# Hybrid attention and SwiGLU block on one core: attention steps of the first three groups taken in pairs on TensorE

## The chip, the cores and the metric

The kernel runs on one core of one Trainium2 chip. The metric is device time in microseconds (us) of that core. The changes are judged against the median of three runs of the kernel before, and the profile is one execution of the program on the chip.

## What is computed

The reference applies one layer to `x` (512 tokens, 2048 features): a sparse attention mixer with a residual, then a SwiGLU feed-forward with a residual. Cut to what matters here:

```python
h = rms_norm(x, norm_mix_g)
proj = h @ w_in                       # 16 query heads of 128, 6 x 4 key/value heads, gates
for each group g of 4, each of its 4 heads, each branch (selected, window), each tile of 128 queries:
    s = q @ k.T * scale               # causal, so tile t has (t + 1) * 128 keys
    p = softmax(masked s) * gate
    o += p @ v                        # the compressed branch is added to the same sum
x = x + concat(o) @ w_out
h = rms_norm(x, norm_ffn_g)
x = x + (silu(h @ w_gate) * (h @ w_up)) @ w_down
```

With 512 tokens all 8 selection blocks are taken, so the selected branch is plain causal attention with its own keys and values. A product in float32 is written as three products of float32r parts: `mm3` multiplies high by high, high by low and low by high part.

## The kernel before

Five engines run their own programs, written out by hand and bound together by semaphores. TensorE (PE) does all products and the transposes, ScalarE (ACT) makes the high parts (`copy`), the exponentials and the copies of results, VectorE (DVE) makes the low parts (`lo`), maxima and weights, SyncE (SP) loads the weights, GpSimd (POOL) takes inverse roots.

The attention part runs over four groups, and each group over 32 steps (`STEPS`), i = 0 to 31: head i // 8, branch i // 4 % 2, query tile t = i % 4. The names used below, for step i:

- **S(i)**, `scores(i)`: the product of queries and keys into PSUM bank 2 + i % 2, three matmuls of 256 to 512 columns. For t = 0 one call serves both branches, so S(i) with i % 8 == 4 issues nothing.
- **max(i)**, `maximum(i)` on DVE: mask, maximum and a copy into `pbuf` (two halves, i % 2). **exp(i)**, `probs(i)` on ACT: the exponential in `pbuf` and its row sum. **weigh(i)**, `weigh(i)` on DVE: three small instructions on `wgt` and `pbuf`, which let the transposes go (`p_ready`).
- **T(i)**, the transposes on PE: t + 1 tiles of `pbuf` into bank 4 + i % 2, in full float32.
- **pth(i)** on ACT and **ptl(i)** on DVE, both named `pt_part(i)`: high and low part of the transposed tiles. Where t = 0 and i is 4 or more, pth(i) waits for `pv_done`, since the values of the branch before still read the buffer `pth`.
- **V(m)**, `values(m)` on PE: the products with the values for the four tiles of branch m, 12 matmuls and one more for an even m.
- **F(w)**, `filler(w)`: in the first three groups half a unit of the next group's projection, which gives PE work while the other engines run. A half with w of 8 or more is 12 matmuls of 512 columns. The table `FILL_P` gives them to the steps. Steps with i % 4 == 1 (from 5 on) have none: V(i // 4 - 1) stands there.
- `keys_sums`, `keys_bcast`, `queries_sums`: the norms of the next group's keys and queries, issued at the steps `KSUM_AT`, `KB_AT`, `KB2_AT`, `QSUM_AT`. DVE takes the results in `keys_den`, `keys_diag`, `keys_norm` and `queries_den`, one step off these.

On PE a step is: V if i % 4 == 1, the fillers, at i % 8 == 0 four transposes of `pc` (compressed branch), T(i), S(i + 2), then sums or broadcasts. On DVE the turn i of the loop is: weigh(i - 1), at i % 8 == 2 a part of `ptc`, ptl(i - 2), max(i), at i % 8 == 7 a product for the compressed branch (`compressed_thrice`), outputs of the projection and a weight split (`splits`). On ACT it is: exp(i), pth(i - 1), the same outputs and splits. Each engine runs its list in order, so an instruction that waits holds all behind it. ptl(i) also waits until S(i + 2) is done.

The two lines that set who waits for the values are in ACT's `pt_part`:

```python
if i >= TT and i % TT == 0:
    wait(act, pv_done, i // TT, 2 * REP, g)
```

Of the kernel before, what the change touches and what calls it, by code (L numbers as in the profile page):

```python
# [4 lines left out]
P = 128  # L5
S, D = 512, 2048
HEADS, GROUPS, DH = 16, 4, 128
REP = HEADS // GROUPS
CMP_LEN, CMP_STRIDE = 32, 16
N_CMP = (S - CMP_LEN) // CMP_STRIDE + 1  # L10
CPAD = 32
# [6 lines left out]
TT = S // P  # L18
# [107 lines left out]
LAST = GROUPS - 1  # L126
# [12 lines left out]
    + [[42], [43], [], [], [44], [45]]  # L139
TAIL_A, END_A = [46], 47  # L140

KSUM_AT, KB_AT, KB2_AT, QSUM_AT, KSPLIT_AT = 13, 17, 19, 26, STEPS - 2


assert S // SEL_BLOCK <= N_SELECT and WINDOW >= S
# [4 lines left out]
def nsa_swiglu_block(nc, x, mix_g, ffn_g, w_in, b_gate, q_g, k_g, cmp_pos, cmp_w1, cmp_b1, cmp_w2,  # L150
# [5 lines left out]
    with ctx:  # L156
# [104 lines left out]
        def bank(b):  # L261
            return ps[:, b, :]
# [58 lines left out]
        def wait(eng, s, base, per=0, i=0):  # L321

            eng.wait_ge(s, i * per + base if per else base)
# [30 lines left out]
                self.local, self.per, self.i = 0, 0, 0  # L354

        WARM = 14
        H_BANKS = [0, 1, 2, 3, 4, 5, 6, 7, 2, 3, 4, 5, 6, 7, 2, 3]
# [654 lines left out]
        def _(dve):  # L1014
# [211 lines left out]
            def attention(g, fill, tail, last):  # L1226
# [90 lines left out]
                def maximum(i):  # L1317
                    nk = (i % TT + 1) * P
                    e, m = slice(i % 2, i % 2 + 1), i // (2 * TT) * TT + i % TT
                    first = 0 if i % TT else (2 + i // TT % 2) * P  # L1320
                    nc.vector.tensor_tensor_reduce(pbuf[:, i % 2, 0:nk], bank(2 + i % 2)[:, first:first + nk], causal[:, S - nk:],  # L1321
                                                   nrq[:, m:m + 1], 3e38, ALU.add, ALU.min, nb[:, e]).then_inc(nb_ready, 1)
# [27 lines left out]
                    for q in range(3, OWN // 2):  # L1350
                        first_out(q)
                for i in range(1, STEPS + 2):
                    if i <= STEPS:
                        weigh(i - 1)
                    if i % 8 == 2:
                        wait(dve, ptc_hi, i // 8 + 1, REP, g)
                        at = ptc[2 * CPAD:, :]
                        lo(at, bank(0)[2 * CPAD:3 * CPAD, :], at, ptc_ready)
                    if i >= 2:
                        pt_part(i - 2)  # L1360
                    if i < STEPS:
                        maximum(i)
                    if i == 1:
                        compressed_weigh()
                        splits(ended(HEAD_FILL))
                    if i % 8 == 7 and i < STEPS - 1:
                        compressed_thrice(i // 8 + 1)
                    if i < 2:
                        continue
                    j = i - 2  # L1370
                    if last and j:
                        staged_added(after(j - 1))
                    if last and j >= 8 and j % 8 == 0:
                        dve.wait_ge(own_hi, j // 8)
                        lo(hTl[:, OWN + j // 8 - 1, :], bank(1), hTh[:, OWN + j // 8 - 1, :], own_lo)
                    if not last:
                        for part, half in part_halves(fill, j):
                            part_out(g + 1, part, half)
                    splits(after(j))
                    if last:  # L1380
                        continue
                    if j == 3:
                        dve.wait_ge(cs_done, g + 1)
                        compressed_keys(g + 1)
                    if j == KSUM_AT - 1:
                        keys_den(g + 1)
                    if j == KSUM_AT:
                        keys_diag(g + 1)
                    if j == KB_AT - 1:
                        keys_norm(g + 1, 0)  # L1390
                    if j == KB2_AT - 1:
                        keys_norm(g + 1, 1)
                    if j == QSUM_AT - 1:
                        queries_den(g + 1, 0)
                    if j == KSPLIT_AT:
                        keys_split(g + 1)
# [275 lines left out]
        def _(pe):  # L1672
            def mm(out_, a, b, start=False, stop=False):
                return nc.tensor.matmul(out_, a, b, start=start, stop=stop, skip_group_check=True)  # L1674
# [160 lines left out]
            def keys_sums(p):  # L1835

                wait(pe, ksq_ready, 2, 2, p)
                for j in range(8):
                    last = mm(bank(0)[:, j:j + 1], sq[:, j // TT, j % TT * P:(j % TT + 1) * P], inv128[:, 0:1], True, True)
                last.then_inc(ksum_done, 1)  # L1840

            def keys_bcast(p, b):

                wait(pe, kdiag_ready, 1, 1, p)
                if b:
                    wait(pe, k_norm, 1, 2, p)
                for t in range(TT):
                    last = mm(bank(0)[:, t * P:(t + 1) * P], inv128[:, :], diag[:, b * TT + t, :], True, True)
                last.then_inc(kb_done, 1)

            def queries_sums(p, h0):

                wait(pe, qsq_ready, h0 + 2, 4, p)
                for h in (h0, h0 + 1):
                    for t in range(TT):
                        last = mm(bank(0 if h0 == 0 else 5)[:, h * TT + t:h * TT + t + 1], sq[:, h - h0, t * P:(t + 1) * P],
                                  inv128[:, 0:1], True, True)
                last.then_inc(qsum_done, 1)
# [26 lines left out]
            def attention(g, fill, tail, last_group):  # L1885
# [54 lines left out]
                def filler(w, tiles=(0, 1)):  # L1940
                    u, half = w // 2, w % 2
                    if u == 0:
                        wait(pe, q_lo, 3 + half, 4, g)
                    if not last_group:
                        proj_half(u, half, P_UNITS, g + 1, g + 1)
                        return
                    c, q = u // 3, u % 3
                    if half == 0 and 0 in tiles:
                        arrive(A0 + u)
                        if c == 0:  # L1950
                            pe.wait_ge(ot_lo, 2 * q + 2)
                    if q == 0 and c:
                        pe.wait_ge(x2_staged, 2 * (c - 1) + half + 1)
                    tokens_half(A0 + u, q, half, 6 + half, 12, tiles)
# [10 lines left out]
                compressed_scores()  # L1965
                for w in HEAD_FILL[0 if last_group else 2:]:
                    filler(w)
                for i in range(STEPS):
                    t = i % TT
                    if i > TT and t == 1:  # L1970
                        values(i // TT - 1)
                    for w in fill[i]:
                        filler(w)
                    if last_group and i == STEPS - 1:
                        filler(tail[0], (0,))
                    if i % 8 == 0:
                        h = i // 8
                        wait(pe, pc_ready, h + 1, REP, g)
                        if h:
                            wait(pe, ptc_ready, h, REP, g)  # L1980
                        if not last_group and h == 2:
                            wait(pe, k_den, 1, 1, g + 1)
                        if not last_group and h == 3:
                            wait(pe, k_norm, 2, 2, g + 1)
                        for tt in range(TT):
                            last = nc.tensor.transpose(bank(0)[0:3 * CPAD, tt * P:(tt + 1) * P],  # L1986
                                                       pc3[:, tt, :, :].rearrange("p r c -> p (r c)"), ident[:, :])
                        last.then_inc(trc_done, 1)
                    wait(pe, p_ready, i + 1, STEPS, g)
                    if i == 1:  # L1990
                        wait(pe, q_den, 2, 2, g)
                    if i >= 2:
                        wait(pe, pt_lo, i - 1, STEPS, g)
                    for k in range(t + 1):
                        ks = slice(k * P, (k + 1) * P)
                        last = nc.tensor.transpose(bank(4 + i % 2)[:, ks], pbuf[:, i % 2, ks], ident[:, :])  # L1996
                    last.then_inc(tr_done, 1)
                    if i + 2 < STEPS:
                        scores(i + 2)
                    if last_group:  # L2000
                        continue
                    if i == KSUM_AT:
                        wait(pe, ptc_ready, KSUM_AT // 8 + 1, REP, g)
                        keys_sums(g + 1)
                    if i == KB_AT:
                        wait(pe, ptc_ready, KB_AT // 8 + 1, REP, g)
                        keys_bcast(g + 1, 0)
                    if i == KB2_AT:
                        keys_bcast(g + 1, 1)
                    if i == QSUM_AT:  # L2010
                        wait(pe, ptc_ready, QSUM_AT // 8 + 1, REP, g)
                        queries_sums(g + 1, 0)
                for w in tail:
                    filler(w, (1,) if last_group else (0, 1))
                values(2 * REP - 1)
# [136 lines left out]
```

## Time and profile before

| | |
|---|---|
| time, median of 3 runs | 2195.71 us (2193.26 to 2196.3) |
| profiled execution: its own time | 2192.59 us |
| profiled execution: span | 2190.6 us |
| PE busy | 2176.8 us (99%) |
| DVE busy | 1557.3 us (71%) |
| ACT busy | 1038.0 us (47%) |
| mean granted TensorE clock | 0.997 |

The span runs from the first to the last instruction. The steps of attention run from about 260 to 850 us, some 145 us for a group. A busy PE is not a PE at its peak: matmuls overlap, so a record is longer than the time until the next one starts. What a matmul costs in a stream is the distance between two starts. A releaser in brackets names the instruction that ended an idle time.

### The profile page before, as it was taken

To read this page: it belongs to the slowest core of one execution; us is meant where nothing else is said; L and a number is where in the kernel's file an instruction comes from. 1 tells how busy PE (TensorE), PEld (TensorE's weight loads), DVE (VectorE), ACT (ScalarE), POOL (GpSimd) and SP (SyncE) were. 2 spreads that over 40 slices of the span, in tenths; PEclk is the share of its full clock that TensorE was granted. 3 is DMA by queue.
4 is the path that set the end of the run, shared out by engine and by line. 5 is a ranking of instruction groups with operands and counts; after the bars stand their busy time and mean duration, and the time that the engine had idled before them with its cause. 6 is when DMAs were issued, how large, how long until landed. Compare 5 with 4: busy or idle time off the path is not lost.

```text
span 2190.6 us, 30130 instructions
## 1 busy us (share of the span) xinstructions
PE 2176.8 (99%) x11377; PEld 1867.0 (85%) x11377; DVE 1557.3 (71%) x2261; ACT 1038.0 (47%) x1482; POOL 101.1 (5%) x115
## 2 busy tenths in 40 slices
PE   9999999999999999999999999999999999999999
PEld 7898988989889998788888888888888888888887
DVE  6333466575666554798777777777877898989898
ACT  5332345343444333864445445445444565555553
POOL 1000000000001000100000000000000000000000
PEclk9999999999999999999999999999999999999999
DMA  5342212212214222644655555455465677666545
GB/s 177 116 116 87 78 59 59 68 49 67 60 59 145 68 68 81 208 164 122 179 162 161 154 165 178 120 163 178 131 175 163 185 225 237 192 192 197 174 143 164
DMA packets 209071, 300.49 MB, mean 137 GB/s; under 512 B 16588, under 2 KB 116209, under 8 KB 207521
## 3 DMA queue, kind: packets, MB, share of 16 engines
q1 hardware_dynamic: 197522, 255.40, 35.8%
q0 software_dynamic: 11408, 43.20, 9.5%
q8 instruction: 90, 1.47, 0.3%
q14 instruction: 51, 0.42, 0.1%
HBM read 235.35 MB, written 28.57 MB: 120 GB/s over the span
## 4 chain that ended last, share of the span: by engine, by line
PE 95%; DVE 2%; ACT 1%; issue 1%; DMA 0%; POOL 0%; SPq 0%; DVEq 0%; ACTq 0%
PE ps L1674 92%; PE ps L1996 1%; PE ps L2066 1%; DVE wl L1019 0%; DVE hTl L1019 0%; ACT wh L616 0%; DMA x_rows<-in_x_dram 0%; DVE x_rows L1051 0%; ACT left_val L865 0%; PE ps L1986 0%; PE ps L2031 0%; DVE ptl L1344 0%; DVE pbuf L1321 0%; ACT pbuf L768 0%; ACT sq L900 0%
## 5 line engine op out<-in xcount | busy, mean ns | idle before, releaser
L616 ACT ACTIVATE wh<-g 128x1024 fp32r<-128x1024 f32 x462 | 489.7, 1061 | 574.4 <-PE ps L1674 433.4
L1019 DVE TENSOR_TENSOR wl<-g,wh 128x1024 fp32r<-128x1024 f32 x462 | 564.5, 1222 | 225.2 <-PE ps L1674 217.4
L1674 PE MATMUL ps<-wh,left_hi 128*128 128x512 f32 x1232 | 481.7, 391 | 0.8 <-DVE wl L1019 0.5
L1674 PE MATMUL ps<-wh,left_lo 128*128 128x512 f32 x1232 | 479.7, 389 | 0.0
L1674 PE MATMUL ps<-wl,left_hi 128*128 128x512 f32 x1232 | 479.3, 389 | 0.0
L1674 PEld LDWEIGHTS ps<-wh,left_hi 128*128 128x128 f32 x1232 | 231.3, 188 | 49.3 <-issue 1.4
L1674 PEld LDWEIGHTS ps<-wh,left_lo 128*128 128x128 f32 x1232 | 231.3, 188 | 48.4
L1674 PEld LDWEIGHTS ps<-wl,left_hi 128*128 128x128 f32 x1232 | 231.4, 188 | 47.2
L1674 PE MATMUL ps<-wh,down_hi 128*128 128x512 f32 x616 | 239.8, 389 | 0.0
L1674 PE MATMUL ps<-wh,down_lo 128*128 128x512 f32 x616 | 239.7, 389 | 0.0
L1674 PE MATMUL ps<-wl,down_hi 128*128 128x512 f32 x616 | 239.6, 389 | 0.0
L1019 DVE TENSOR_TENSOR wl<-raw,wh 128x1024 fp32r<-128x1024 f32 x122 | 148.9, 1222 | 122.0 <-ACT wh L616 119.4
L1674 PE MATMUL ps<-hTh,wh 128*128 128x512 f32 (+1 forms) x560 | 215.4, 385 | 1.7 <-DVE wl L1019 1.0
L1674 PE MATMUL ps<-hTh,wl 128*128 128x512 f32 (+1 forms) x560 | 212.1, 379 | 0.0
L1674 PE MATMUL ps<-hTl,wh 128*128 128x512 f32 (+1 forms) x560 | 211.6, 378 | 0.0
L1674 PE MATMUL ps<-wh,hTh 128*128 128x256 f32 (+1 forms) x704 | 210.1, 298 | 0.7 <-DVE hTl L1019 0.3
L1674 PE MATMUL ps<-wl,hTh 128*128 128x256 f32 (+1 forms) x704 | 207.8, 295 | 0.0
L1674 PE MATMUL ps<-wh,hTl 128*128 128x256 f32 (+1 forms) x704 | 207.7, 295 | 0.0
L616 ACT ACTIVATE wh<-raw 128x1024 fp32r<-128x1024 f32 x122 | 128.8, 1059 | 125.5 <-PE ps L1674 106.2
L1674 PEld LDWEIGHTS ps<-wh,hTh 128*128 128x128 f32 x704 | 136.6, 194 | 6.0 <-issue 3.5
L1674 PEld LDWEIGHTS ps<-wh,hTl 128*128 128x128 f32 x704 | 136.6, 194 | 2.5
L1674 PEld LDWEIGHTS ps<-wl,hTh 128*128 128x128 f32 x704 | 136.7, 194 | 2.4
(214 smaller groups left out, 2985.5 us busy)
## 6 DMA issues: line engine op xcount, KB each, us to landing
g<-in_ffn_w_gate_dram SPq DMA_DIRECT2D x176, 256.0 KB, 3.1
g<-in_ffn_w_up_dram SPq DMA_DIRECT2D x176, 256.0 KB, 4.2
g<-in_ffn_w_down_dram SPq DMA_DIRECT2D x176, 256.0 KB, 4.9
raw<-in_nsa_w_in_dram SPq DMA_DIRECT2D x164, 256.0 KB, 3.0
g<-g POOLq DMA_DIRECT2D x66, 512.0 KB, 4.9
down_val<-m_scratch SPq DMA_DIRECT2D x77, 256.0 KB, 4.7
raw<-in_nsa_w_out_dram SPq DMA_DIRECT2D x64, 256.0 KB, 3.1
m_scratch<-work SPq DMA_DIRECT2D x22, 384.0 KB, 2.9
```

The source lines that it names most:

```text
L616: return nc.scalar.activation(dst, src, ACT.Copy)
L1019: nc.vector.tensor_tensor(dst, src, hi.bitcast(f32), ALU.subtract).then_inc(done, 1)
L1674: return nc.tensor.matmul(out_, a, b, start=start, stop=stop, skip_group_check=True)
L1996: last = nc.tensor.transpose(bank(4 + i % 2)[:, ks], pbuf[:, i % 2, ks], ident[:, :])
L2066: last = nc.tensor.transpose(bank(2 * spare + k)[:, tt * P:(tt + 1) * P], src, ident[:, :])
```

## The change

In the first three groups (`paired(g)`) PE takes two steps together: for an even i it issues T(i), T(i + 1), S(i + 2), S(i + 3), and an odd step keeps only its values and fillers. The last group stays as it is. The sums and broadcasts of the next group now stand ahead of the transposes of their step, three of them a step later. A broadcast (`keys_bcast`) is one matmul call of 512 columns where it was four of 128. On DVE, in odd turns i from 3 on, weigh(i - 1) moves from the head of the turn to behind ptl(i - 2) and max(i). ACT's program stays.

```diff
-KSUM_AT, KB_AT, KB2_AT, QSUM_AT, KSPLIT_AT = 13, 17, 19, 26, STEPS - 2
+KSUM_AT, KB_AT, KB2_AT, QSUM_AT, KSPLIT_AT = 14, 18, 20, 26, STEPS - 2
...
+        def paired(g):
+            return g != LAST
...
                 for i in range(1, STEPS + 2):
-                    if i <= STEPS:
+                    weigh_last = paired(g) and 2 < i < STEPS and i % 2
+                    if i <= STEPS and not weigh_last:
                         weigh(i - 1)
...
                     if i < STEPS:
                         maximum(i)
+                    if weigh_last:
+                        weigh(i - 1)
...
-                for t in range(TT):
-                    last = mm(bank(0)[:, t * P:(t + 1) * P], inv128[:, :], diag[:, b * TT + t, :], True, True)
-                last.then_inc(kb_done, 1)
+                mm(bank(0), inv128[:, :], diag[:, b * TT:(b + 1) * TT, :].rearrange("p j c -> p (j c)"), True, True)\
+                    .then_inc(kb_done, 1)
...
+                def next_group_sums(i):
+                    if i in (KSUM_AT, KB_AT, QSUM_AT):
+                        wait(pe, ptc_ready, i // 8 + 1, REP, g)
+                    if i == KSUM_AT:
+                        keys_sums(g + 1)
+                    if i == KB_AT:
+                        keys_bcast(g + 1, 0)
+                    if i == KB2_AT:
+                        keys_bcast(g + 1, 1)
+                    if i == QSUM_AT:
+                        queries_sums(g + 1, 0)
...
                     if i % 8 == 0:
...
+                        compressed_transposes(i // 8)
+                    if not last_group:
+                        next_group_sums(i)
+                    if not paired(g):
+                        transposes(i)
+                        if i + 2 < STEPS:
+                            scores(i + 2)
+                    elif i % 2 == 0:
+                        transposes(i)
+                        transposes(i + 1)
+                        if i + 2 < STEPS:
+                            scores(i + 2)
+                            scores(i + 3)
```

`compressed_transposes` and `transposes` hold the instructions and waits that stood in the loop before.

PE, steps 8 to 10 of a group, before: the four `pc` transposes, T(8), S(10), V(1) (the `pth` and `ptl` rows), T(9), S(11), then the filler of step 10 (its 12 rows left out) and T(10).

```order
L1996 MATMUL ps<-ident,pbuf 128x128 [waits pt_lo,p_ready]
L1674 MATMUL ps<-kh,qh 128x384 [waits nb_ready]
...
L1674 MATMUL ps<-pth,vh 128x512 [waits pt_lo]
...
L1674 MATMUL ps<-pth,vl 128x128
L1996 MATMUL ps<-ident,pbuf 128x128 [waits pt_lo,p_ready]
L1996 MATMUL ps<-ident,pbuf 128x128
L1674 MATMUL ps<-kh,qh 128x512 [waits nb_ready]
...
L1996 MATMUL ps<-ident,pbuf 128x128 [waits pt_lo,p_ready]
L1996 MATMUL ps<-ident,pbuf 128x128 x2
```

The same stretch with the change: T(8) and T(9) in a row (one tile and two), S(10), S(11), V(1), the filler of step 10 (left out), T(10), T(11).

```order
L2006 MATMUL ps<-ident,pbuf 128x128 [waits pt_lo,p_ready] x2
L2006 MATMUL ps<-ident,pbuf 128x128
L1680 MATMUL ps<-kh,qh 128x384 [waits nb_ready]
...
L1680 MATMUL ps<-kh,qh 128x512 [waits nb_ready]
...
L1680 MATMUL ps<-pth,vh 128x512 [waits pt_lo]
...
L1680 MATMUL ps<-pth,vl 128x128
...
L2006 MATMUL ps<-ident,pbuf 128x128 [waits pt_lo,p_ready]
L2006 MATMUL ps<-ident,pbuf 128x128 x2
L2006 MATMUL ps<-ident,pbuf 128x128 [waits pt_lo,p_ready]
L2006 MATMUL ps<-ident,pbuf 128x128 x3
```

T(9) and S(11) moved from behind V(1) to ahead of it, and T(11) now follows T(10) without a filler between them.

DVE, turns 10 and 11, before: ptl(8), max(10) (the two ISA rows), a split, weigh(10), ptl(9), max(11), weigh(11).

```order
L1344 TENSOR_TENSOR ptl<-ps,pth 128x128 [waits s_done,pt_hi]
L1321 ISA pbuf,nb<-ps,causal,nrq 128x384
L1019 TENSOR_TENSOR wl<-raw,wh 128x1024 [waits hi_ready]
L1329 TENSOR_SCALAR wgt<-sums 128x1 [waits exp_done]
L1331 RECIPROCAL wgt<-wgt 128x1 [waits vector_done]
L1336 TENSOR_SCALAR pbuf<-pbuf,wgt,gates_g 128x384 [waits vector_done]
L1344 TENSOR_TENSOR ptl<-ps,pth 128x2x128 [waits s_done,pt_hi]
L1321 ISA pbuf,nb<-ps,causal,nrq 128x512
...
L1336 TENSOR_SCALAR pbuf<-pbuf,wgt,gates_g 128x512 [waits vector_done]
```

The same turns with the change.

```order
L1347 TENSOR_TENSOR ptl<-ps,pth 128x128 [waits s_done,pt_hi]
L1324 ISA pbuf,nb<-ps,causal,nrq 128x384
L1022 TENSOR_TENSOR wl<-raw,wh 128x1024 [waits hi_ready]
L1347 TENSOR_TENSOR ptl<-ps,pth 128x2x128 [waits s_done,pt_hi]
L1324 ISA pbuf,nb<-ps,causal,nrq 128x512
L1332 TENSOR_SCALAR wgt<-sums 128x1 [waits exp_done]
L1334 RECIPROCAL wgt<-wgt 128x1 [waits vector_done]
L1339 TENSOR_SCALAR pbuf<-pbuf,wgt,gates_g 128x384 [waits vector_done]
...
L1339 TENSOR_SCALAR pbuf<-pbuf,wgt,gates_g 128x512 [waits vector_done]
```

ptl(9) and max(11) moved ahead of weigh(10); weigh(11) follows directly.

DVE, turn 21, with the change: the second normalisation of the keys (`kst`), which waits for the second broadcast, stands between weigh(20) (one tile) and weigh(21) (two tiles).

```order
L1339 TENSOR_SCALAR pbuf<-pbuf,wgt,gates_g 128x128 [waits vector_done]
L1022 TENSOR_TENSOR wl<-raw,wh 128x1024 [waits hi_ready]
L1163 TENSOR_TENSOR kst<-kst,ps 128x512 [waits kb_done,kst_ready]
L1332 TENSOR_SCALAR wgt<-sums 128x1 [waits exp_done]
L1334 RECIPROCAL wgt<-wgt 128x1 [waits vector_done]
L1339 TENSOR_SCALAR pbuf<-pbuf,wgt,gates_g 128x256 [waits vector_done]
```

Before, the same `kst` row stood ahead of both, with a filler between T(20) and T(21) on PE. Now PE issues the broadcast right ahead of T(20) and T(21).

## Rows read from the trace of the kernel before

**Rows 1.** The page, its first line.

```profile
span 2190.6 us, 30130 instructions
```

**Rows 2.** Waits, 260 to 850 us: total, times, longest.

```profile
ACT pth L616 <- PE ps L1674: 82.9, 28, 6.4
...
PE ps L1996 <- DVE pbuf L1336: 2.2, 2, 1.4
```

**Rows 3.** Timeline of group 1, steps 8 and 9: start, duration, instruction, count.

```profile
435.66 0.60 PE L1986 MATMUL ps<-ident,pc 128*96 128x128 f32 x4
436.09 0.27 PE L1996 MATMUL ps<-ident,pbuf 128*128 128x128 f32 x1
...
436.38 0.34 PE L1674 MATMUL ps<-kl,qh 128*128 128x384 f32 x1
...
438.60 0.41 PE L1996 MATMUL ps<-ident,pbuf 128*128 128x128 f32 x2
...
439.08 0.39 PE L1674 MATMUL ps<-kl,qh 128*128 128x512 f32 x1
```

**Rows 4.** The same timeline, from the end of V(1) to weigh(11).

```profile
438.49 0.28 PE L1674 MATMUL ps<-pth,vl 128*128 128x128 f32 x1
...
438.86 0.28 ACT L616 ACTIVATE pth<-ps 128x128 fp32r<-128x128 f32 x1 [1.97 <-PE ps L1674]
...
439.38 0.61 DVE L1321 CUSTOM_DVE_ANT_0 pbuf<-ps,causal,nrq 128x384 f32<-128x384 f32 x1
...
439.54 0.39 PE L1674 MATMUL ps<-hTh,wh 128*128 128x512 f32 x1
...
440.46 0.62 ACT L768 ACTIVATE pbuf<-pbuf,nb 128x384 f32<-128x384 f32 x1
...
441.06 0.38 ACT L616 ACTIVATE pth<-ps 128x256 fp32r<-128x256 f32 x1
...
441.26 0.15 DVE L1329 TENSOR_SCALAR wgt<-sums 128x1 f32<-128x1 f32 x1
...
441.64 0.48 DVE L1336 TENSOR_SCALAR pbuf<-pbuf,wgt,gates_g 128x384 f32<-128x384 f32 x1
...
442.03 0.42 DVE L1344 TENSOR_TENSOR ptl<-ps,pth 128x256 fp32r<-128x256 f32 x1
...
442.28 0.49 PE L1996 MATMUL ps<-ident,pbuf 128*128 128x128 f32 x3
442.37 0.74 DVE L1321 CUSTOM_DVE_ANT_0 pbuf<-ps,causal,nrq 128x512 f32<-128x512 f32 x1
...
443.15 0.72 ACT L768 ACTIVATE pbuf<-pbuf,nb 128x512 f32<-128x512 f32 x1 [1.71 <-DVE nb L1321]
...
444.00 0.15 DVE L1329 TENSOR_SCALAR wgt<-sums 128x1 f32<-128x1 f32 x1 [0.88 <-ACT pbuf L768]
...
444.39 0.54 DVE L1336 TENSOR_SCALAR pbuf<-pbuf,wgt,gates_g 128x512 f32<-128x512 f32 x1
```

**Rows 5.** Timeline, other places: a broadcast, its reader, sums, an idle time of PE.

```profile
475.92 1.05 PE L1674 MATMUL ps<-sq,inv 128*128 128x128 f32 x8
...
477.08 0.69 DVE L1160 TENSOR_TENSOR kst<-kst,ps 128x512 f32<-128x512 f32 x1 [1.94 <-PE ps L1674]
...
499.92 1.84 PE L1674 MATMUL ps<-inv,sq 128*128 128x1 f32 x16
...
832.59 0.55 PE L1996 MATMUL ps<-ident,pbuf 128*128 128x128 f32 x3 [1.36 <-DVE pbuf L1336]
```

**Rows 6.** Tile `kcg`: count, duration min/median/max in ns, first and last start.

```profile
L1674 PE MATMUL ps<-kcg,qh x64: 195/277/402, 247.7 to 669.4; 128*128 128x64 f32 x64
```

**Rows 7.** Windows: length, PE, PEld, DVE, ACT, POOL busy, granted clock, DMA share, GB/s.

```profile
393.00:396.00 3.00, 3.00 (x16) 3.00 (x16) 2.83 (x6) 0.00 (x0) 0.00 (x0) 0.50 0.00 0
...
532.00:535.00 3.00, 3.00 (x28) 3.00 (x28) 0.45 (x3) 0.09 (x1) 0.00 (x0) 1.00 0.00 0
669.00:676.00 7.00, 6.69 (x33) 6.61 (x33) 5.30 (x14) 1.44 (x3) 4.30 (x2) 0.51 0.34 98
```

More of the change, by code:

```diff
@@ L1967, in attention, with compressed_transposes, transposes @@
                     filler(w)
+                def compressed_transposes(h):
+                    wait(pe, pc_ready, h + 1, REP, g)
+                    if h:
+                        wait(pe, ptc_ready, h, REP, g)
+                    if not last_group and h == 2:
+                        wait(pe, k_den, 1, 1, g + 1)
+                    if not last_group and h == 3:
+                        wait(pe, k_norm, 2, 2, g + 1)
+                    for tt in range(TT):
+                        last = nc.tensor.transpose(bank(0)[0:3 * CPAD, tt * P:(tt + 1) * P],
+                                                   pc3[:, tt, :, :].rearrange("p r c -> p (r c)"), ident[:, :])
+                    last.then_inc(trc_done, 1)
+                def next_group_sums(i):
[9 more added lines that the diff above has]
+                        queries_sums(g + 1, 0)
+                def transposes(i):
+                    wait(pe, p_ready, i + 1, STEPS, g)
+                    if i == 1:
+                        wait(pe, q_den, 2, 2, g)
+                    if i >= 2:
+                        wait(pe, pt_lo, i - 1, STEPS, g)
+                    for k in range(i % TT + 1):
+                        ks = slice(k * P, (k + 1) * P)
+                        last = nc.tensor.transpose(bank(4 + i % 2)[:, ks], pbuf[:, i % 2, ks], ident[:, :])
+                    last.then_inc(tr_done, 1)
                 for i in range(STEPS):
-                    t = i % TT
-                    if i > TT and t == 1:
+                    if i > TT and i % TT == 1:
                         values(i // TT - 1)
@@ L1976, in attention @@
                     if i % 8 == 0:
[L1977 to L2009, printed above, removed]
@@ L2010, in attention @@
-                    if i == QSUM_AT:
-                        wait(pe, ptc_ready, QSUM_AT // 8 + 1, REP, g)
-                        queries_sums(g + 1, 0)
+                        compressed_transposes(i // 8)
[11 more added lines that the diff above has]
+                            scores(i + 3)
```

## The prediction

> **What bounds the kernel now.** I read the page first: PE is busy for nearly all of the span [rows 1] (the table above has the shares). So time is won or lost only where PE's stream gets shorter or stops. The waits come next. In the whole attention stretch PE's matmuls stood for only 2.2 us because of DVE's weighed `pbuf` [rows 2], two times; 1.36 of it is at 832.59, in the last group [rows 5], which doesn't change. In the three groups that do change, the chains of ACT and DVE are hidden behind fillers. The question is whether they stay hidden. Here one row counts: ACT waits 82.9 us, 28 times, for PE's products before a `pth` copy [rows 2], and 438.86 is one of these waits [rows 4]. The copy pth(8) starts 0.37 behind the last matmul of V(1), as the code says. It costs nothing today, but the chain that begins there ends in T(10). Weigh(10) ends at 441.64 + 0.48 = 442.12 and PE reaches T(10) at 442.28 [rows 4]. The cover is only 0.16 us thick.
>
> **What pairing saves.** From the first `pc` transpose to the second matmul of S(10) are 0.72 us. Less 0.17 for 384 columns, five transposed tiles cost 0.55; T(8) alone costs 0.12, T(9) (two tiles) 0.48 - 0.23 = 0.25 [rows 3]. So a tile is 0.11 and a change between transposes and float32r products some 0.02. Merging 1 + 2 tiles saves at most 0.05 (0.12 + 0.25 against 0.32), and 3 + 4 about nothing. With 16 pairs in 3 groups that is 0 to 2.4 us. Sums and broadcasts merged with transposes save the same 0.02 each, 12 times. I take 1.5 in all.
>
> The broadcast: eight records (two per float32 matmul) last 1.05, the last start 0.79 behind the first, so some 0.11 a record and 0.9 a broadcast [rows 5]. Afterwards two records stream 512 columns each. At the price per column of now that is 0.9 again. The bounds are 0.23 a record (a float32r matmul of 512, which is two starts apart in the filler of rows 4, 2.74 for 12) and twice the present price: 8 broadcasts of 0.46 to 1.8 us, so -3.5 to +7 us. I take 0, the row nearest by data type. The Trainium skill, in FP8 and Floating Point Precision, TensorE Precision Notes, says that true FP32 makes four passes through the array. By that the price is an estimated 4 x 512 / 2.4 GHz = 0.85 us a broadcast, 0.4 us won over eight; no run here shows the wide form yet.
>
> **What pairing costs.** I put zero at the start of V's last matmul (438.49 for V(1)) and lay out the new order from there with the distances of [rows 4].
>
> PE's due time: V ends at 0.11, one filler follows (439.54 to 442.28, 2.74), nothing else. T(10) is due at 2.85. Today T(9) and S(11) lie between (438.60 to 439.54, 0.94 us), and T(10) is due at 3.79. The change has spent them ahead of V.
>
> The chain to T(10): pth(8) 0.37, max(10) 0.89, exp(10) 1.97 (ACT first makes a split and a head's output), pth(9) 2.57 and done at 2.95. All this is as now. Now weigh(10) would come next (2.77). In the new order DVE first waits for pth(9): ptl(9) 3.0, max(11) 0.34 later, 3.34, and weigh(10) behind it about 0.7 later, at 4.0. The last of its three instructions starts 0.38 later and takes 0.48: 4.9. T(10) starts at 4.9 and PE has stood 2.05.
>
> The chain to T(11), which is now due right behind T(10): exp(11) starts 0.78 behind max(11), 4.1; its weigh 0.85 later, 5.0; the last part at 5.35, 0.54 long: 5.9. T(10) took 0.33 from 4.9, so PE stands 0.7 again. Together 2.75 us. Before, T(11) had a filler of 2.74 ahead of it.
>
> All seven pairs that start at i = 6, 10, ... 30 have this form: V, an empty step, one filler. Three things vary. Without split and head output exp(i) starts as soon as its maximum is ready (0.78 - 0.13 behind it, since 384 columns take 0.61 against 0.74), at 1.54 instead of 1.97. In turns 7, 15 and 23 DVE makes a product of 384 columns before the second weigh, which I estimate at 0.5 from instructions of that size. And sums (1.8 us, [rows 5]) or a broadcast (0.9) now stand between the filler and T at 14, 18 and 26 and fill the gap; at 18 the `kst` product (0.69) delays the second weigh.
>
> - 6: due 2.85, T(6) at 4.5, T(7) at 5.8; PE stands 1.6 + 1.0
> - 10: 2.05 + 0.7
> - 14: due 4.65, 4.7 and 6.1; 0.0 + 1.1
> - 18: due 3.75, 4.9 and 6.35; 1.2 + 1.1
> - 22: 4.6 and 5.9; 1.7 + 1.0
> - 26: due 4.65, 4.9 and 5.9; 0.3 + 0.7
> - 30: 4.5 and 5.5; 1.6 + 0.7
>
> The sum is 14.8 us a group. The other pairs (4, 8, 12, ...) have two fillers, 5.5 us, ahead of them: the same chains end 0.1 to 2 us before the due time, nearest at T(17) and T(3). One of them breaks for another reason. In turn 21 `kst` waits for the second broadcast, as it does now for 1.94 at 477.08 [rows 5], and weigh(21) is behind it. PE issues the broadcast (0.9), T(20) (0.12) and then T(21). DVE's product can start about 0.2 behind the broadcast and takes 0.69, weigh(21) 0.38 + 0.41: T(21) is some 1.6 late. That gives 16.4 us a group, 49 us for three.
>
> **The clock.** At each group's start PE issues 32 small matmuls of 64 and 32 columns [rows 6], starts near 388, 531 and 666 in the stretch here. They last 3.6 us. After the first and third the granted clock fell to 0.50 and 0.51, the lower level (1.2 GHz); after the second it stayed at full [rows 7]. The falls cost 1.5 us or more in the first and 0.49 x 7 = 3.4 in the second. A pause of 1.36 us in the last group (832.59, [rows 5]) was too short to compare. The new pauses with the seven tiles between them make stretches of some 3.1 to 3.7 us in which PE streams even less than in those 3.6. There are 7 a group, 21. Two in three fell in the sparse stretches seen, but the new ones touch full streams on both sides and several are shorter. I choose 8 falls at 2.5 us, 20 us, between 0 and 21 x 3.4 = 71.
>
> **The sum.** 2192.6 (own time of the profiled execution) - 1.5 + 49 + 20 = 2260. The median of the runs is 3 us above that execution: 2263.
>
> **Rivals.**
>
> - *Pauses, but no falls of the clock* (0.30). Speaks for it: the longest single pause is 2.1 us, and one sparse stretch in three did nothing. Against it: PE wasn't idle at all when the clock fell. 2243 us. The Trainium skill, TensorE: Matmul & The Clock Gate, Why this matters for your kernels, asks only that pauses between bursts stay below a length that none of mine reaches; by that rule this is the outcome. The trace doesn't bear it out: two sparse stretches without a pause were enough.
> - *Half the pauses* (0.10). If the hardware overlaps the three parts of a weigh or the copy with more than the rows show, each link is shorter. One link of 1 us less in seven pairs takes 2 x 7 x 3 x 0.5 = 21 us away: 2210 to 2226.
> - *Not slower* (0.09). The mechanism: pth(4k) goes on right behind T(4k) and not behind V. The place is ACT's turn 4k + 1. V is 2 us and S(i + 2), S(i + 3) about 1 us, so the whole chain would start 3 us earlier and T(10) be ready at 1.9, against a due time of 2.85. Only the 1.5 us saved would remain: 2194. The point from which it decides is a chain that is 2.1 us shorter. Against it: the wait in the code and 28 such waits in the trace. With the cheap end of the broadcast it would be faster, 2190.
> - *More falls than I chose* (within the forecast's case): 15 falls of 2.5 give 2280.
>
> **Chances and range.** Pauses with falls of the clock 0.51, 2252 to 2290; pauses alone 0.30; half pauses 0.10; not slower 0.09, of it 0.04 faster. A difference of 0.2% (4.4 us) is about what these runs can tell from none. The likeliest case gives 2263. The range from 2225 to 2288 leaves out the 0.09, some of the half pauses and the tail of many falls. Slower 0.91, same 0.05, faster 0.04.
>
> **What would show it.** In the new trace PE's idle time before the transposes of `pbuf` rises from 2.2 to some 50 us, released by DVE's `pbuf`, seven times a group before three tiles, seven before four, and once before two (T(21)). Timeline: T(10) some 4.9 behind V(1)'s last matmul. Windows: clock values near 0.5 right behind such pauses. The transposes themselves keep 0.11 a tile. In the last group nothing changes.
>
> **What would make it wrong.** Starts of T(10) at the due time would kill the chain; I should then look at how ACT's copy was released. An idle time of 50 us with a clock of 1.00 makes it 2243. A broadcast of 1.8 us would add up to 7 us.

## The result and the profile after

| | before | after |
|---|---|---|
| median of the runs, us | 2194.49 (2192.74 to 2196.30, 4 runs) | 2262.12 (2259.17 to 2267.61, 4 runs) |
| profiled execution, its span, us | 2192.59, 2190.6 | 2260.39, 2258.4 |
| mean granted clock | 0.997 | 0.989 |

The change makes the kernel slower by 3.1%: the ratio is 1.031, with a 95% interval from 1.0297 to 1.0323. The span grew by 67.8 us.

The page of the changed kernel, its first line and the shares of the chain that ended last:

```profile
span 2258.4 us, 30034 instructions
...
PE 90%; DVE 5%; ACT 3%; issue 1%; DMA 0%; POOL 0%; SPq 0%; DVEq 0%; ACTq 0%
```

Before, PE held 95% of that chain, DVE 2% and ACT 1%. So the chain runs through DVE and ACT for five points more of the span. That is more than the time in which PE stands, because the chain also follows them while PE still works at a filler. Where PE stands is in the waits of the changed kernel, 260 to 920 us (total, times, longest):

```profile
ACT pth L619 <- PE ps L1680: 123.6, 28, 7.4
...
PE ps L2006 <- DVE pbuf L1339: 44.7, 50, 1.8
```

These answer to [rows 2]. PE's wait for the weighed `pbuf` went from 2.2 us in two waits to 44.7 us in fifty, and ACT's wait ahead of `pth` from 82.9 to 123.6 in the same 28 waits. The timeline of group 0, steps 8 to 11 (the pattern of [rows 4], a group earlier), shows how one would lead to the other (the experiments test it):

```profile
303.44 0.27 PE L1680 MATMUL ps<-pth,vl 128*128 128x128 f32 x1
...
303.81 0.28 ACT L619 ACTIVATE pth<-ps 128x128 fp32r<-128x128 f32 x1 [2.87 <-PE ps L1680]
...
306.01 0.38 ACT L619 ACTIVATE pth<-ps 128x256 fp32r<-128x256 f32 x1
...
306.43 0.42 DVE L1347 TENSOR_TENSOR ptl<-ps,pth 128x256 fp32r<-128x256 f32 x1
...
306.77 0.74 DVE L1324 CUSTOM_DVE_ANT_0 pbuf<-ps,causal,nrq 128x512 f32<-128x512 f32 x1
...
307.82 0.48 DVE L1339 TENSOR_SCALAR pbuf<-pbuf,wgt,gates_g 128x384 f32<-128x384 f32 x1
...
308.35 0.55 PE L2006 MATMUL ps<-ident,pbuf 128*128 128x128 f32 x3 [1.84 <-DVE pbuf L1339]
...
308.79 0.55 DVE L1339 TENSOR_SCALAR pbuf<-pbuf,wgt,gates_g 128x512 f32<-128x512 f32 x1
309.39 0.65 PE L2006 MATMUL ps<-ident,pbuf 128*128 128x128 f32 x4 [0.49 <-DVE pbuf L1339]
```

Read it from V(1)'s last matmul at 303.44. pth(8) starts 0.37 later, pth(9) 2.57 later, T(10) 4.91 and T(11) 5.95 later. The idle figure in brackets begins at the modelled end of the last matmul; from start to start a pause is some 0.2 us longer.

Other places of group 0: weigh(4), a weight split and weigh(5) on DVE with T(5), then T(6) and T(7), and then the second broadcast with T(20), its reader and T(21):

```profile
280.98 0.35 DVE L1339 TENSOR_SCALAR pbuf<-pbuf,wgt,gates_g 128x128 f32<-128x128 f32 x1
...
281.60 1.23 DVE L1022 TENSOR_TENSOR wl<-raw,wh 128x1024 fp32r<-128x1024 f32 x1 [0.27 <-ACT wh L619]
...
283.29 0.41 DVE L1339 TENSOR_SCALAR pbuf<-pbuf,wgt,gates_g 128x256 f32<-128x256 f32 x1
...
283.76 0.44 PE L2006 MATMUL ps<-ident,pbuf 128*128 128x128 f32 x2 [0.52 <-DVE pbuf L1339]
...
291.72 0.55 PE L2006 MATMUL ps<-ident,pbuf 128*128 128x128 f32 x3 [1.42 <-DVE pbuf L1339]
...
293.03 0.66 PE L2006 MATMUL ps<-ident,pbuf 128*128 128x128 f32 x4 [0.77 <-DVE pbuf L1339]
...
349.98 1.02 PE L1680 MATMUL ps<-sq,inv 128*128 128x512 f32 x2
350.84 0.27 PE L2006 MATMUL ps<-ident,pbuf 128*128 128x128 f32 x1
351.11 0.69 DVE L1163 TENSOR_TENSOR kst<-kst,ps 128x512 f32<-128x512 f32 x1 [1.28 <-PE ps L1680]
...
352.10 0.41 DVE L1339 TENSOR_SCALAR pbuf<-pbuf,wgt,gates_g 128x256 f32<-128x256 f32 x1
352.56 0.44 PE L2006 MATMUL ps<-ident,pbuf 128*128 128x128 f32 x2 [1.45 <-DVE pbuf L1339]
```

The windows that answer to [rows 7] (same columns; with the counts in brackets left aside, the sixth number behind the length is the granted clock, 0.50 being 1.2 GHz). The first two rows are a pause of group 0 and the start of group 1, the third is the start of group 2, the fourth a pause of group 2:

```profile
324.00:328.00 4.00, 3.16 (x16) 2.73 (x17) 2.47 (x9) 1.85 (x5) 1.63 (x1) 0.73 0.31 106
...
414.00:421.00 7.00, 7.00 (x37) 7.00 (x37) 4.54 (x13) 0.63 (x1) 0.00 (x0) 0.54 0.00 0
...
578.00:585.00 7.00, 7.00 (x37) 7.00 (x37) 4.67 (x13) 0.63 (x1) 0.00 (x0) 0.53 0.00 0
720.00:725.00 5.00, 3.74 (x13) 3.02 (x14) 4.25 (x9) 3.71 (x7) 0.00 (x0) 0.68 0.01 3
```

I read such windows of 2 us from 240 to 930 us and summed length times (1 - clock), which I call the clock loss below. Before it is 5.1 us in two falls, after 23.9 us in ten. Six falls stand at pauses (near 325, 395, 472, 558, 636, 720) and cost 1.7 us each, four stand at group starts (near 250, 414, 578, 734) and cost 3.4 each.

The second sum that I use is PE's time in transposes, sums and broadcasts from 264 to 1000 us: start of the float32r matmul behind such a stretch less start of the one before it, less the usual distance of that matmul. Pauses are in it. It was 67.7 us and is 123.0: 55.3 more, part of it run at the low clock. The other 12.5 of the 67.8 us lie in the float32r work at the low clock.

### The profile page after: what moved, and what is told of

Same layout as the page of the kernel before. It is cut to its first block, busy times and chain, and to the rows that moved or that the text cites. A ratio compares the mean times of both kernels' runs of the same rounds, so it can differ in the third digit from the quotient of the medians.

```text
span 2258.4 us, 30034 instructions
## 1 busy us (share of the span) xinstructions
PE 2203.1 (98%) x11329; PEld 1878.7 (83%) x11329; DVE 1560.4 (69%) x2261; ACT 1038.5 (46%) x1482; POOL 101.1 (4%) x115
## 4 chain that ended last, share of the span: by engine, by line
PE 90%; DVE 5%; ACT 3%; issue 1%; DMA 0%; POOL 0%; SPq 0%; DVEq 0%; ACTq 0%
PE ps L1680 87%; PE ps L2006 2%; ACT wh L619 1%; DVE pbuf L1339 1%; PE ps L2083 1%; DVE pbuf L1324 1%; ACT pbuf L771 1%; DVE wl L1022 1%; DVE ptl L1347 0%; ACT pth L619 0%; DVE wgt L1334 0%; DVE hTl L1022 0%; DMA x_rows<-in_x_dram 0%; DVE x_rows L1054 0%; ACT left_val L868 0%
## 5 line engine op out<-in xcount | busy, mean ns | idle before, releaser
L1347 DVE TENSOR_TENSOR ptl<-ps,pth 128x128 fp32r<-128x128 f32 (+2 forms) x160 | 64.8, 422 | 156.1 <-ACT pth L619 143.0
```

Source lines behind the costliest of these rows:

```text
L1347: last_ = nc.vector.tensor_tensor(dst, src, hi.bitcast(f32), ALU.subtract)
```

## The experiments

My theory was that the loss comes from pauses ahead of late pairs plus falls of the clock, and that pauses come from the order on three engines. The rivals were that the falls alone or the sums and broadcasts matter, and that only one of the two new orders (PE's or DVE's) does. Ratios are against the kernel before.

**double_buf.** A second pair of `pth` and `ptl` buffers in groups 0 and 1, so that the copy pth(4k) no longer waits for V; group 2 keeps one pair as a control.

```diff
...
-                    if i >= TT and i % TT == 0:
-                        wait(act, pv_done, i // TT, 2 * REP, g)
+                    if i >= (2 * TT if g < 2 else TT) and i % TT == 0:
+                        wait(act, pv_done, i // TT - (g < 2), 2 * REP, g)
...
```

> The changed kernel with a second buffer for the transposed tiles (pth, ptl) in groups 0 and 1, so that the copy pth(4k) waits for the values of two branches back, V(k - 2), and not for V(k - 1); group 2 keeps one buffer and is the control. My theory (V holds ACT's copy, the copy holds the chain to the next two transposes): in groups 0 and 1 the pauses before pairs 6, 14, 22 and 30 vanish; those before 10 and 18 shrink to some 1.6 and 1.2 us, since ACT still waits for V(k - 1) before a head's output; that before T(21) (broadcast) stays 1.6. That is some 12 us a group less and up to four falls of the clock less (1.7 each): 2232 against 2262 now. The rival that DVE's own load and order make the pauses: no change in any group, 2262.

2235.44 us, ratio 1.0189 (1.0172 to 1.0206); clock loss 15.4. Timeline, PE's transposes:

```profile
287.60 0.93 PE L2013 MATMUL ps<-ident,pbuf 128*128 128x128 f32 x7
...
302.00 0.55 PE L2013 MATMUL ps<-ident,pbuf 128*128 128x128 f32 x3 [0.67 <-DVE pbuf L1345]
303.04 0.66 PE L2013 MATMUL ps<-ident,pbuf 128*128 128x128 f32 x4 [0.49 <-DVE pbuf L1345]
...
318.73 0.66 PE L2013 MATMUL ps<-ident,pbuf 128*128 128x128 f32 x4 [0.71 <-DVE pbuf L1345]
...
334.87 0.65 PE L2013 MATMUL ps<-ident,pbuf 128*128 128x128 f32 x4 [1.34 <-DVE pbuf L1345]
```

At 6 (287.60), 22 and 30 the seven tiles run in one piece: the buffer's wait was the whole cause there, and 26.7 us of the 67.6 came back, with the wait removed in two groups of three. Group 2, the control, kept all its pauses. At 14, 18 and 26 a pause ahead of the second step of the pair stayed. I had not foreseen these.

**db_full.** The same, and in all of the first three groups ACT makes a head's output one turn later and DVE the second `kst` product one turn later.

```diff
-                    if j >= 8 and j % 8 == 0:
+                    if last and j >= 8 and j % 8 == 0:
                         head_out(j // 8 - 1)
+                    if not last and j >= 8 and j % 8 == 1:
+                        head_out(j // 8 - 1)
...
-                    if j == KB2_AT - 1:
+                    if j == KB2_AT:
```

> As double_buf, and in the first three groups the head's output on ACT stands one turn later (behind pth(8h + 1)) and the second normalisation of the keys on DVE one turn later (behind weigh(21)). My theory: the pauses before 10, 18 and T(21) go too; left are some 1.3 us a group before T(3) and T(25) in groups 0 and 1, group 2 with 15 us, and the falls of the clock at the group starts: 2220. The rival: no change to the changed kernel, 2262.

2226.68 us, ratio 1.0143 (1.0126 to 1.016). In groups 0 and 1 T(10) and T(21) no longer wait. The miss is 7 us; the three pauses at 14, 18 and 26 are there again (0.71 to 1.37 of idle time), with falls of the clock beside two of them in group 0 and one in group 1 (clock loss 18.8). The two small pauses that the expectation puts ahead of T(3) and T(25) are those of T(5) and T(29): in the changed kernel they are the row at 283.76 and its like at 385.16, and both have two tiles.

**weigh_first.** PE's pairs stay, DVE keeps its order of before.

```diff
-                    weigh_last = paired(g) and 2 < i < STEPS and i % 2
+                    weigh_last = False
```

> The changed kernel with DVE's old order (weigh(i - 1) always at the head of the turn). My theory: the first transpose of a bad pair is ready 1.2 us earlier and the second 0.5 us later, and the second decides: some 2 us a group more, 2267. The rival that the moved weigh makes the pauses: 2240 or less.

2280.92 us, ratio 1.0395 (1.0378 to 1.0412). Timeline around T(6) and T(7):

```profile
286.22 0.36 ACT L619 ACTIVATE pth<-ps 128x256 fp32r<-128x256 f32 x1
...
287.13 0.42 DVE L1347 TENSOR_TENSOR ptl<-ps,pth 128x256 fp32r<-128x256 f32 x1
287.27 0.55 PE L2006 MATMUL ps<-ident,pbuf 128*128 128x128 f32 x3
287.47 0.74 DVE L1324 CUSTOM_DVE_ANT_0 pbuf<-ps,causal,nrq 128x512 f32<-128x512 f32 x1
...
290.09 0.66 PE L2006 MATMUL ps<-ident,pbuf 128*128 128x128 f32 x4 [2.27 <-DVE pbuf L1339]
```

T(6) is nearly on time, but max(7) now stands behind weigh(6), and T(7) waits 2.27. PE's stretches of transposes grew by 10 us and the clock loss by 8.5: one long pause in place of two short ones. The direction was right, the size too small: the fall of the clock was not in my figure. DVE's new order is a help for the pairs, not a cause of the loss.

**pair_first and pair_second.** Only the pairs (4k, 4k + 1), or only (4k + 2, 4k + 3); the other steps go one by one.

```diff
-                    weigh_last = paired(g) and 2 < i < STEPS and i % 2
+                    weigh_last = paired(g) and 2 < i < STEPS and i % TT == 1
...
-                    if not paired(g):
+                    if not paired(g) or i % TT // 2 != 0:
```

(3 and 1 in pair_second.)

> Only the pairs (4k, 4k + 1) are taken together, the steps 4k + 2 and 4k + 3 as before, with the old order of DVE in their turns. My theory: T(4k + 2) is due 0.94 us earlier than before and ready at 3.2 to 3.65 instead of being covered: pauses of 0.35, 0.8, 0.5 and 0.35 us before T(6), T(10), T(22), T(30), none at 14, 18, 26, 1.6 before T(21): some 4.2 us a group, 2207, and up to 8 us more if the clock falls at the group starts as in the changed kernel. The rival that any pairing costs alike: half of the changed kernel's loss, 2228.

2221.06 us, ratio 1.0117 (1.01 to 1.0134).

```profile
283.07 0.44 PE L2006 MATMUL ps<-ident,pbuf 128*128 128x128 f32 x2 [1.40 <-DVE pbuf L1339]
```

This is T(5). I expected T(21) to be the only late step of these pairs. In each group T(5), T(13), T(17), T(25) and T(29) wait too, 0.35 to 1.6 from start to start, and a group's pauses are 8.2 and not 4.2. S(4k + 1) goes singly here, so only one filler is left between it and T(4k + 1). The pauses that I had foreseen came: 0.3, 0.8, 0.3 and 0.3 at T(6), T(10), T(22) and T(30), and 1.6 at T(21). The result is 14 us above my figure, and the pairs' cover depends on the neighbour being paired too.

> Only the pairs (4k + 2, 4k + 3) are taken together. My theory: T(4k + 2) is due at 3.8 behind V and ready at 4.5 to 4.9, T(4k + 3) 0.7 to 1.1 behind it: 8 us a group, and 0.7 before T(3): 27 us, 2221, and up to 10 us more for falls of the clock. With pair_first the two sum to less than the whole loss, because the 0.94 us that the first pair takes away only hurts where the second has no cover. The rival that each pairing costs alike: 2228.

2230.25 us (2221.45 to 2232.28), ratio 1.0149 (1.0131 to 1.0167). The losses of the halves, 26 and 36 us, add to 62, near the 68 of the whole. The pauses are 9 to 10 us a group, a little over the 8 foreseen (none of them at T(5), which isn't paired here), and the profiled execution has a clock loss of 17.1. The lowest of the four executions, 2221.45, ran at a mean granted clock of 0.998, the other three, 2229.97 to 2232.28, at 0.992 and 0.993. The same program can thus come out some 9 us shorter or longer, and the clock goes with it.

**v_early.** V(k - 1) stands behind the fillers of step 4k and ahead of T(4k), not behind S(4k + 3): PE does the same work and frees the buffer earlier.

```diff
-                    if i > TT and i % TT == 1:
+                    if last_group and i > TT and i % TT == 1:
                         values(i // TT - 1)
...
+                    if not last_group and i >= TT and i % TT == 0:
+                        values(i // TT - 1)
...
                     if i % 8 == 0:
                         compressed_transposes(i // 8)
```

> The changed kernel with V(k - 1) ahead of T(4k) in step 4k instead of behind the pair in step 4k + 1, so that pth(4k) has nothing to wait for; buffers and DVE as changed. My theory: the chain starts right behind T(4k), against one filler as before: T(4k + 2) ready some 0.6 us late and T(4k + 3) another 0.7, 1.3 instead of 2.7 us a bad pair, 1.6 before T(21) stays: 7 to 9 us a group, 2218 to 2225 with fewer falls. The rival that not the place of V but DVE's load decides: 2262.

2231.69 us, ratio 1.0171 (1.0156 to 1.0187); clock loss 8.5. Moving V alone gives back 30 us. T(10) and T(11), T(19) and T(21) of group 0:

```profile
303.78 0.55 PE L2006 MATMUL ps<-ident,pbuf 128*128 128x128 f32 x3 [0.88 <-DVE pbuf L1339]
304.82 0.66 PE L2006 MATMUL ps<-ident,pbuf 128*128 128x128 f32 x4 [0.49 <-DVE pbuf L1339]
...
336.49 0.66 PE L2006 MATMUL ps<-ident,pbuf 128*128 128x128 f32 x4 [1.13 <-DVE pbuf L1339]
...
347.55 0.44 PE L2006 MATMUL ps<-ident,pbuf 128*128 128x128 f32 x2 [1.45 <-DVE pbuf L1339]
```

From start to start 1.3 to 1.7 stayed at 6, 10, 22 and 30 (1.3 foreseen), 0.9 to 1.3 at 14, 18 and 26, and 1.6 at T(21); T(5) and T(29) no longer wait. That makes 10 to 11 us a group where I had 7 to 9.

**before_woven.** The kernel before, with the 32 small matmuls at a group's start [rows 6] mixed into the next filler, two at a time.

```diff
+            woven = []
...
+                last = mm(out_, a[1], b[0], stop=stop)
+                for _ in range(min(2, len(woven))):
+                    woven.pop(0)()
+                return last
...
```

> The kernel before, with the 32 small matmuls of compressed_scores mixed one pair at a time, two pairs behind each triple, into the filler that follows them, so that no stretch of small matmuls alone is left at a group's start. The theory that these sparse stretches bring the clock down: the two falls (5 us by the clock row) vanish, 2189 to 2190, 0.2% faster. The rival that the falls have another cause or come back elsewhere: no change.

2200.67 us, ratio 1.0028 (1.0017 to 1.004): wrong. Timeline and window of the last group's start:

```profile
669.19 0.55 PE L1674 MATMUL ps<-wh,hTh 128*128 128x256 f32 x1 [4.24 <-DVE hTl L1019]
```

```profile
668.00:685.00 17.00, 15.81 (x74) 15.84 (x75) 6.29 (x15) 1.44 (x3) 4.23 (x2) 0.51 0.19 66
```

The first filler of the last group was not ready. The small matmuls had covered that; now PE stands 4.24 us, and they are spread over a stretch of 17 us at the low clock. The fall near 392 was not seen.

**woven_three.** The same, but in the last group the small matmuls are issued together as before.

```diff
+                while last_group and woven:
+                    woven.pop(0)()
```

> As before_woven, but in the first three groups only; the last group has its 32 small matmuls in one piece again, where they hide the wait of its first filler for a low part of the hidden columns. The fall of the clock near 392 goes (1.7 us), the one near 669 stays, the wait of 4.2 us that before_woven laid bare is covered again: 2192 to 2193, at the edge of what can be measured. If the mixing itself costs: above 2195.

2191.76 us (11 runs) against 2194.66 (21 runs), ratio 0.9988 (0.9979 to 0.9997); clock loss 3.4, one fall. It is 0.12% faster than the kernel before, and the interval only just leaves out no change. That mixing keeps the clock up is likely and not proved: at the first three group starts the two woven traces show no fall in six places, and before, bcast_only and sums_moved five in nine, but such falls come and go between executions (below).

**bcast_only and sums_moved.** The first is the kernel before with the wide broadcast; the second the changed kernel with no group paired.

```diff
         def paired(g):
-            return g != LAST
+            return False
```

> The kernel before with the broadcast as one matmul call of 512 columns, nothing else. At 0.86 us against 0.90, as the changed kernel's rows have it, eight broadcasts save 0.3 us: no difference that can be measured. The rival that the wide form helps or hurts elsewhere (a longer hold of the bank, another clock): over 2 us either way.

> The changed kernel with no group paired: only the broadcast as one call and the sums and broadcasts ahead of the transposes of their step are left of the change. My theory that the loss is all in the pairs: 2194, no difference that can be measured. The rival that the place of the sums carries part of it: 2200 or more.

2194.19 us, ratio 1.0 (0.9991 to 1.0009), and 2192.28 us, ratio 0.9993 (0.9983 to 1.0002). In sums_moved the wait is back at its old size, so the whole loss is in the pairs, their order on DVE included:

```profile
PE ps L2006 <- DVE pbuf L1339: 2.2, 2, 1.4
```

**readers_late.** The changed kernel; the four DVE instructions of each group that read the sums and broadcasts stand behind the second weigh of their pair and no longer between the two.

```diff
+                    if paired(g) and i == KSUM_AT + 2:
+                        keys_den(g + 1)
+                    if paired(g) and i == KB_AT + 2:
+                        keys_norm(g + 1, 0)
+                    if paired(g) and i == KB2_AT + 2:
+                        keys_norm(g + 1, 1)
+                    if paired(g) and i == QSUM_AT + 2:
+                        queries_den(g + 1, 0)
...
```

The same calls are taken out at the end of the turns.

> The changed kernel with the four DVE instructions that read the sums and broadcasts (keys_den, keys_norm twice, queries_den) moved from the end of turns 15, 19, 21, 27, where they stand between the two weighs of a pair, to right behind the second weigh, in turns 16, 20, 22, 28. The second theory (such a reader waits for a product that PE issues right ahead of the same pair, and holds the second weigh): the pause before T(21), 1.65 us a group, goes; those at T(15), T(19), T(27) shrink little, because there the chain from V is late anyway. 5 us less, 2257, if the clock's falls stay as they are.

2257.15 us, ratio 1.0285 (1.0269 to 1.0301). The figure was met, though not by its working alone: the pauses shrank by some 2 us a group, and the clock loss grew from 23.9 to 27.3. T(20) and T(21) now run together behind the broadcast:

```profile
351.13 1.02 PE L1680 MATMUL ps<-sq,inv 128*128 128x512 f32 x2
351.99 0.49 PE L2006 MATMUL ps<-ident,pbuf 128*128 128x128 f32 x3
```

At 14, 18 and 26 the second step still waits, 0.9, 0.65 and 0.65 from start to start, against 1.0, 1.05 and 0.65 in the changed kernel.

**db_readers.** Both: second buffers in groups 0 and 1, the head's output a turn later and the readers late in all three.

> Second buffer in groups 0 and 1, a head's output a turn later and the readers behind the second weigh. In db_full, in groups 0 and 1, 0.9 us stood before T(15), 1.55 before T(19), 0.9 before T(27), 0.7 before T(3). Second theory: the first three go, and with them the falls of the clock near them: 7 us and some 5 us less than db_full, 2215. If the rest of these pauses has another cause: 2226.

2217.14 us, ratio 1.0101 (1.0086 to 1.0117). The pairs at 14 and 18 of group 0:

```profile
315.86 0.96 PE L2015 MATMUL ps<-ident,pbuf 128*128 128x128 f32 x7
...
330.42 0.93 PE L2015 MATMUL ps<-ident,pbuf 128*128 128x128 f32 x7
```

Both mechanisms together clear the pairs at 6, 10, 14, 18, 22, 26 and 30 of groups 0 and 1; the short pauses at T(5) and T(29) remain, and most of group 2's (13.6 us from start to start, with five of the eight falls of the clock between 577 and 680).

## Why the prediction came out as it did

**What pairing saves** (1.5 us): right. Seven tiles in a row take 0.765 us from float32r to float32r, three and four apart 0.335 + 0.445, so 0.015 is won; with one and two tiles it is 0.03. Over 48 pairs that is 0.7 to 1.4 us.

**The broadcast** (0): right. The two records take 0.86 us (349.98 to T(20) at 350.84) against 0.9 for eight. The Trainium skill, FP8 and Floating Point Precision, TensorE Precision Notes, puts true FP32 at four passes, an estimated 0.85; the trace agrees. bcast_only shows that it doesn't move the time.

**The chains to T(10) and T(11)** (4.9 and 5.9 behind V(1)'s last matmul): 4.91 and 5.95. From start to start the pauses of group 0 are 2.6 at 6, 2.8 at 10, 1.15 at 14, 2.25 at 18, 2.6 at 22, 1.0 at 26, 3.0 at 30 (partly at the low clock), and 1.7 at T(21). Each is within 0.1 of its figure but the one at 30, where 2.3 was predicted; there the two pauses are 1.6 and 0.65, as laid out, and the rest is work at the low clock. That the wait for V starts the chain is shown by double_buf and v_early; that the `kst` product makes T(21) late, by readers_late and db_full.

**The other pairs** ("end 0.1 to 2 us before the due time, nearest at T(17) and T(3)"): this step was wrong in the small. T(3) and T(17) did not wait, but PE stood 0.7 us at T(5) and 0.55 at T(29) from start to start, places that the prediction does not name. Before, S(4k + 2) and V(k - 1) stood between T(4k) and T(4k + 1). Now T(5) follows T(4), and on DVE the weight split of 1.23 us at 281.60 stands between weigh(4) and weigh(5); at T(29) it is one at 383.17. That the split is what makes them late is read from the rows and not tested. The pauses stay in db_readers and go in v_early, where V leaves more time between S(4k + 1) and T(4k + 1). A group costs 17 to 18 us, not 16.4.

**A cause counted but not seen.** At 14, 18 and 26 my sum put the pauses ahead of the second step down to the one chain from V. double_buf took V away and they stayed, at 0.9, 1.5 and 0.9 from start to start; readers_late took away the readers alone, and they stayed too; db_readers took away both, and they went. So there are two chains of nearly the same length. The prediction had the instructions in its turns, so its sizes came out, but it would have been wrong on what a second buffer wins.

**The clock** (8 more falls at 2.5, 20 us): 8 more, 18.8 us. The sum is right for reasons that are only half mine, and so in part by luck. At the 21 pairs there were 6 falls at 1.7 us, 10.2. The rest is at group starts, 13.6 against 5.1 before. And that part isn't all the change's doing. Here are the windows of group 0's start, before and after. Ahead of it the change has only given group 0's own broadcasts their wide form:

```profile
248.00:260.00 12.00, 12.00 (x103) 12.00 (x103) 8.63 (x24) 3.63 (x7) 0.00 (x0) 1.00 0.01 1
```

```profile
248.00:260.00 12.00, 12.00 (x78) 12.00 (x78) 8.12 (x23) 2.67 (x6) 0.00 (x0) 0.72 0.00 1
```

Eleven traces have these same instructions up to here; six show this fall (after, pair_first, pair_second, readers_late, bcast_only, sums_moved) and five don't. So 3.4 us of the profiled difference may be this execution's. Whether the pauses made the falls at the three later group starts more likely stays open: after the change the clock fell at all three, in before, bcast_only and sums_moved, which have no pairs, at two of the three. Of the nine traces with pairs seven show all three, weigh_first two and v_early one, 24 of 27 against 6 of 9. That leans to a part of the pauses in it and does not prove one.

**The rivals.** Pauses without falls (2243) is refuted: the clock fell beside pauses whose single idle times are below 1.9 us. The Trainium skill, TensorE: Matmul & The Clock Gate, Why this matters for your kernels, asks for short pauses between bursts; by that rule alone the six falls wouldn't be there, and the trace disagrees. Half the pauses and no loss are refuted by the timeline. As a balance, 3 x 17.5 of pauses less 1.3 plus 18.8 of clock makes 70, against 67.8 measured. The 2 us too many are probably counted twice, since a window at the low clock also holds time in which PE stands.

## What to carry to other kernels

Ahead of moving work on the bounding engine, list for each tile when it is due and when it is ready, through every copy that waits for a buffer and every instruction queued between its producer and its user: 0.16 us of cover was all that hid a chain, and batching that saves 0.03 us a time cost 2.8 there. If such a batch is wanted, free the reused buffer first (a second one, or its reader earlier) and move unrelated readers behind the last producer. Take one late chain away and look again, since a second one of the same length can stand behind it.

## What the runs showed of the hardware

The same instructions at the first group's start (32 small matmuls without a gap) were followed by a fall from 2.4 to 1.2 GHz in six traces and by none in five. The fall cost 3.4 us in two of the six (after, pair_second) and 1.7 in the other four; each of the six beside pauses in the changed kernel cost 1.7. Four executions of pair_second had mean granted clocks of 0.992, 0.993, 0.993 and 0.998, and the last was 9 us the shorter. In before_woven the low clock lasted for 17 us behind a single pause of 4.24 us while the small matmuls were spread over the fillers. In weigh_first 32.3 us were lost to the clock, 8.5 more than with two shorter pauses at the same places.
